# A hybrid decoder layer on eight cores: the first steps of stage2 are moved into the stage3 before it

## The chip, the cores and the metric

The kernel runs on all eight cores of one Trainium2 chip. Each core takes one prompt sequence (2048 tokens, width 1024) and 16 of the 128 sample tokens; the cores exchange nothing. The metric is the device time of the slowest core in microseconds (us).

## What is computed

The layer normalises x (RMS), projects it with w_in, runs a gated linear attention (GLA) branch and a Mamba-2 (SSD) branch over the sequence, merges them with sigmoid gates, applies w_out, adds x and normalises again. Cut to what matters here:

```
hn = rmsnorm(x, norm_g); q,k,v,g,a_lr,z,xbc,dt_raw,gate_a,gate_b = split(hn @ w_in)
log_a = log_sigmoid(a_lr @ w_a2 + b_a2) / 16        # per key channel
o, S = gla_recurrence(q/8, k, v, log_a, S0)         # S_t = diag(a_t) S_{t-1} + k_t^T v_t, o_t = q_t S_t
o = rmsnorm(o) * silu(g)
x_s, B, C = silu(causal_conv(xbc, width 4)); dt = softplus(dt_raw + dt_bias)
y, h = ssd_recurrence(x_s, dt, -exp(a_log), B, C, h0)   # h_t = exp(dt_t A) h_{t-1} + dt_t x_t B_t^T
y = rmsnorm((y + d_skip * x_s) * silu(z))
merged = sigmoid(gate_a) * (o @ w_br_gla) + sigmoid(gate_b) * (y @ w_br_ssd)
out = rmsnorm(x + merged @ w_out)
```

## The kernel before, in words

The 2048 tokens of a core are eight super-chunks (s = 0 to 7) of SC = 256 tokens, each of two chunks (ci = 0, 1) of 128. All of a super-chunk's work lies in generators that record instructions; a `yield` ends a step. The recorded order is the order of each engine's queue (PE, ACT, DVE, POOL, SP), and a wait is added where a named tile was last written or read on another engine. Readers of one PSUM bank (`pb0` to `pb6`) wait for each other too. Nothing is reordered later.

- `stage1a(s)` (L488), 23 steps: for both 128-token tiles the Square of x (ACT), the rstd and xn (POOL), the transposes (PE), xnT (DVE); then the `alr` projection, `wa2`, Exp and Ln to `eb`, the dt projection with its Exp and Ln, `latok` and four scans to `bpos` (DVE, L546), two Exps to `eb` and `enb`, then the k and q projections, each with a product on DVE.
- `stage1b(s)` (L566), 40 steps: six times projection, copy to `xbc_raw` (ACT), convolution in the single buffer `cacc` (four DVE instructions), Silu (ACT): 24 steps; then g and z, four projections with a Silu each: 16 steps.
- `stage2(s)` (L605): `chunk_gen(0)`, then `chunk_gen(1)`, of 8 steps each. Step 1: the V projection, `vtok`, `ktok`, `ccol`. Step 2: cumulative sums over `tri_f` on PE, the differences to `tmp4` and `tg` (eight DVE instructions), Exp to `decay` and `rs`. Step 3: `xdt`, `Btok`, `scm`. Step 4: the two masked products `ATm` (a half of `scrB`). Step 5: the GLA output (`scrB` x `vtok` and `qtT` x `S_bf`, called bo), `sq`, `t1`, the state `S_f`, `S_bf`, and Ln and Exp of the norm in place in a bank (bsg). Step 6: `CsT`, the two `Mg`, `xw`, `ogT`. Step 7: the SSD output (by), y to `tg`, the state `hT_f`. Step 8: the product with z, the norm, `ygT`.
- `stage3_m(s)` (L753), 8 steps (m = 0 to 7): 16 gate and 8 branch matmuls, Tanh to `tg` (ACT), the product (DVE), the sum to `mrgT` (POOL). `tg` is a single buffer.
- `stage3_tail(s)` (L776), 6 steps: two with 16 `wout` matmuls each and the residual on `xr`; then for both tiles the Square and rstd, and the final product with the store of `yp`.

`interleave(gp, gf, rp, rf)` takes rp steps of the first and rf steps of the second in turn. Stage2(s) is woven with tail(s-1) and stage1a(s+1), 1 to 2; stage3(s) with stage1b(s+1), 1 to 5. Ahead of s=0, `late_weights` queues eight weight transfers on POOL, of which each waits for the sixth before it. All matmuls are recorded at L220, transposes at L228, ACT at L234, DVE at L239, L248 and L253, copies at L260, transfers at L272. In the text V is the V projection of chunk 0, and a name with an apostrophe (V', bo', CsT') is the same thing in chunk 1.

Of the kernel before, what the change touches and what calls it, by code (L numbers as in the profile page):

```python
# [9 lines left out]
AF = mybir.ActivationFunctionType  # L10
# [269 lines left out]
def build_program(with_sample=True, stop=None):  # L280
# [18 lines left out]
    with ExitStack() as st:  # L299
# [305 lines left out]
        def stage2(s):  # L605
# [13 lines left out]
            def chunk_gen(ci):  # L619
                sl = slice(ci * 128, (ci + 1) * 128)  # L620
                vn = "vtok%d" % ci
                b, bn = bank(pool=POOL_B)
                k.mmg([(b[:, :], xs_[:, kc, sl], w_in_bf[:, kc, C_V:C_V + 512], kc == 0, kc == 7) for kc in range(8)],
                      wres(C_V, C_V + 512) + [xsn], [bn])
                k.cp("act", vtok[:, ci, :], b[:, :], [bn], [vn])
                ptk = pt[:, 0:256]
                k.trg([(ptk[:, cc * 128:(cc + 1) * 128], k_[:, cc, sl], ident_bf[:]) for cc in range(2)], [kn, "ident_bf"], ["pt"])
                k.cp("act", ktok[:, :], ptk, ["pt"], ["ktok"])
                bc_, bcn = bank(pool=POOL_B)
                k.mmg([(bc_[:, 0:8], tri_f[:, :], la_[:, ci, :], True, True)], ["tri_f", lan], [bcn])  # L630
                k.ts("dve", ccol[:, :], bc_[:, 0:8], -1.0, None, ALU.mult, None, [bcn], ["ccol"])
                yield
                for g in range(2):
                    pr = slice(64 * g, 64 * g + 64)
                    bcu, bcun = bank(pool=POOL_B)
                    bcuv = v4(bcu[:, :], 4)
                    k.mmg([(bcuv[:, hh, :], la_[:, ci, 4 * g + hh:4 * g + hh + 1].broadcast_to([128, 128]), tri_f[:, :], True, True)
                           for hh in range(4)], [lan, "tri_f"], [bcun])
                    for hh in range(4):
                        k.ts("dve", diffs[g][:, hh, :], bcuv[:, hh, :], ccol[:, 4 * g + hh:4 * g + hh + 1], 0.0, ALU.add, ALU.min,  # L640
                             [bcun, "ccol"], [diffn[g]])
                    k.act(decay[:, 4 * g:4 * g + 4, :], diffs[g], AF.Exp, [diffn[g]], ["decay%d" % g])
                    k.act(expcum[pr, :, :], bcuv[pr, :, :], AF.Exp, [bcun], ["rs%d" % g])
                yield
                bx, bxn = bank(pool=POOL_B)
                k.trg([(bx[:, cc * 128:(cc + 1) * 128], x_[:, cc, sl], ident_f[:]) for cc in range(4)], [xsn_, "ident_f"], [bxn])
                k.tt("dve", xdt[:, :, :], bx[:, :].rearrange("p (h q) -> p h q", h=8),
                     dt_[:, ci, :].unsqueeze(2).broadcast_to([128, 8, 64]), ALU.mult, [bxn, dtn], ["xdt"])
                ptb = pt[:, 256:384]
                k.trg([(ptb, B_[:, sl], ident_bf[:])], [Bn, "ident_bf"], ["pt"])  # L650
                k.cp("act", Btok[:, :], ptb, ["pt"], ["Btok"])
                for g in range(2):
                    pr = slice(64 * g, 64 * g + 64)
                    bsc, bscn = bank(pool=POOL_B)
# [37 lines left out]
                k.cp("act", S_bf[:, :, :], S_f[:, :, :], ["S_f"], ["S_bf"])
                bsg, bsgn = bank(hold=True, pool=POOL_B)
                k.mmg([(bsg[:, :], ones_bf[:, :], sq[:, :, :].rearrange("p h i -> p (h i)"), True, True)], ["ones_bf", "sq"], [bsgn])
                k.act(bsg[:, :], bsg[:, :], AF.Ln, [bsgn], [bsgn], scale=1.0 / 128, bias=EPS)
                k.act(bsg[:, :], bsg[:, :], AF.Exp, [bsgn], [bsgn], scale=-0.5)
                yield
                k.tt("dve", CsT[:, :, :], expcum[:, :, :], C_[:, sl].unsqueeze(1).broadcast_to([128, 4, 128]), ALU.mult,
                     ["rs0", "rs1", Cn], ["CsT"])
                for g in range(2):  # L700
                    k.tt("dve", Mgs[g], decay[:, 4 * g:4 * g + 4, :], scm[:, g, :].unsqueeze(1).broadcast_to([128, 4, 128]), ALU.mult,
                         ["decay%d" % g, "scm%d" % g], [Mgn[g]])
                k.tt("dve", xw[:, :, :], xdt[:, :, :], decay[:, :, 127:128].broadcast_to([128, 8, 64]), ALU.mult,
                     ["xdt", "decay0", "decay1"], ["xw"])
                k.tt("dve", ogT[:, :, sl].rearrange("p (cc hh) i -> p hh cc i", hh=2),
                     t1[:, :, :].rearrange("p (hh cc) i -> p hh cc i", hh=2),
                     v4(bsg[:, :], 4).rearrange("p (hh cc) i -> p hh cc i", hh=2), ALU.mult, ["tmp4", bsgn], ["ogT"])
                release(bsgn)
                yield
                bh, bhn = bank(hold=True, pool=POOL_B)  # L710
                bhv = bh[:, 0:256].rearrange("p (h q) -> p h q", h=4)
                for g in range(2):
                    pr = slice(64 * g, 64 * g + 64)
                    by, byn = bank(pool=POOL_B)
                    byv = by[:, 0:256].rearrange("p (c i) -> p c i", c=2)
                    mms = []
                    for hh in range(4):
                        h = 4 * g + hh
                        po = byv[64 * (h % 2):64 * (h % 2) + 64, hh // 2, :]
                        mms.append((po, xdt[:, h, :], Mgs[g][:, hh, :], True, False))  # L720
                        mms.append((po, hT_bf[pr, hh, :], CsT[pr, hh, :], False, True))
# [28 lines left out]
            for ci in range(2):  # L750
                yield from chunk_gen(ci)
# [479 lines left out]
```

How the kernel before makes its waits and increments, by code:

```python
        def replay(ename, eng):  # L155
            mysem = sems[ename]
            for o in ops[ename]:
                for (k, v) in o.waits:
                    eng.wait_ge(sems[k], v)
                if o.dma_key is not None:
                    instrs = o.fn(eng)
                    assert len(instrs) == o.dma_n, (len(instrs), o.dma_n)
                    for ins in instrs:
                        ins.then_inc(sems[o.dma_key], 16)
                elif o.fn is None:
                    eng.nop().then_inc(mysem, 1)
                else:
                    ins = o.fn(eng)
                    ins.then_inc(mysem, 1)
```

## Time and profile before

| | |
|---|---|
| median of 3 runs | 1128.01 us (1125.84 to 1129.49) |
| the profiled execution | 1125.68 us |
| its slowest core (5), span | 1124.1 us; cores 1114.6 to 1124.1 |
| granted PE clock, mean | 0.747 of full |
| busy: PE, PE weight load | 691.3 us (61%), 470.8 us (42%) |
| busy: DVE, ACT, POOL | 497.9 (44%), 312.4 (28%), 153.1 (14%) |
| chain that ended last | PE 39%, DVE 26%, issue 14%, ACT 10%, DMA 5%, POOL 4% |

In time the eight super-chunks fill about 60 to 950 us of the span, the sample batch the rest. The profile in 40 slices (28.1 us each) shows the pattern that repeats:

```profile
PE   0645788468846884688468846884788468140025
DVE  1424552555255525552555255535552442124762
PEclk9965699569956995699569956995699569565557
```

### The profile page before, as it was taken

The page shows a single profiled execution, that of the slowest core. Times are in us where ns is not written, and L with a number is a line of the kernel's source. Part 1 is how long each engine was busy: PE and PEld are TensorE (multiplying, and loading weights), DVE is VectorE, ACT ScalarE, POOL GpSimd, SP SyncE. Part 2 cuts the span into 40 slices and gives each one's busy share as a digit, 9 for nine tenths or more (in the row PEclk, how much of TensorE's full clock was granted, in tenths as well). Part 3 has the DMA queues.
Part 4 walks back from the last instruction along what each step waited for, and adds up shares of the span by engine and source line. Part 5 has one row for each costly group of instructions (what it writes and reads, how often), then busy time and mean ns, then how long its engine had stood idle before and what let it go on. Part 6 is the DMA issues. An engine that isn't in the chain of part 4 may idle for free.

```text
span 1124.1 us, 14666 instructions; the slowest of 8 cores (1114.6 to 1124.1 us)
## 1 busy us (share of the span) xinstructions
PE 691.3 (61%) x4703; PEld 470.8 (42%) x4703; DVE 497.9 (44%) x1029; ACT 312.4 (28%) x662; POOL 153.1 (14%) x232
## 2 busy tenths in 40 slices
PE   0645788468846884688468846884788468140025
PEld 0432476247624752475247624752475245020001
DVE  1424552555255525552555255535552442124762
ACT  1232232332233223322332233323332332020001
POOL 4021210201020102010201020102010002102221
PEclk9965699569956995699569956995699569565557
DMA  9989400300030003000300030002000200401420
GB/s 141 161 102 199 75 2 1 113 1 1 1 112 1 1 1 113 1 1 1 113 0 1 2 112 1 1 1 75 1 1 1 75 6 1 119 18 31 133 75 3
DMA packets 29612, 50.54 MB, mean 45 GB/s; under 512 B 7098, under 2 KB 18973, under 8 KB 29536
## 3 DMA queue, kind: packets, MB, share of 16 engines
q0 software_dynamic: 17968, 22.60, 11.6%
q1 hardware_dynamic: 10160, 22.80, 6.5%
q10 hardware_dynamic: 1408, 4.20, 1.3%
q8 instruction: 39, 0.64, 0.2%
q14 instruction: 37, 0.30, 0.1%
HBM read 50.60 MB, written 13.30 MB: 57 GB/s over the span
## 4 chain that ended last, share of the span: by engine, by line
PE 39%; DVE 26%; issue 14%; ACT 10%; DMA 5%; POOL 4%; DVEq 1%; SPq 1%; ACTq 0%; POOLq 0%
PE pb L220 38%; DVE cacc L253 7%; DMA w_in_bf<-w_in 3%; ACT tg L234 2%; DVE xnT L239 2%; DVE cacc L248 2%; DVE tmp L248 2%; DVE tg L253 1%; ACT sq L234 1%; DVE scrB L239 1%; PE pt L228 1%; POOL sm L239 1%; DVE xr L239 1%; DVEq L159 1%; ACT L234 1%
## 5 line engine op out<-in xcount | busy, mean ns | idle before, releaser
L220 PE MATMUL pb<-xnT,w_in_bf 128*128 128x256 bf16 (+1 forms) x2240 | 316.2, 304 | 50.3 <-ACT gs L234 23.8
L220 PEld LDWEIGHTS pb<-xnT,w_in_bf 128*128 128x128 bf16 (+1 forms) x2240 | 237.6, 108 | 111.1 <-issue 62.3
L253 DVE SCALAR_TENSOR_TENSOR tg<-tg,pb 128x512 f32<-128x512 f32 (+1 forms) x66 | 45.3, 687 | 153.6 <-ACT tg L234 83.3
L239 POOL TENSOR_TENSOR mrgT<-tg 128x256 bf16<-128x256 f32 x64 | 46.8, 732 | 398.0 <-DVE tg L253 393.9
L253 DVE SCALAR_TENSOR_TENSOR cacc<-xbc_raw,prm,cacc 128x256 f32<-128x256 f32 x144 | 77.6, 539 | 15.6 <-DVE cacc L253 0.5
L220 PE MATMUL pb<-scrB,vtok 128*128 128x128 bf16 x64 | 18.0, 281 | 74.1 <-DVE scrB L239 74.1
L234 ACT ACTIVATE tg<-pb 128x512 f32<-128x512 f32 (+1 forms) x68 | 40.1, 590 | 71.5 <-PE pb L220 57.0
L228 PE MATMUL pt<-ident_bf,xn 128*128 128x128 bf16 (+1 forms) x144 | 17.3, 294 | 67.7 <-POOL xn L245 63.0
L220 PE MATMUL pb<-wout,mrgT 128*128 128x512 bf16 x256 | 56.5, 379 | 2.2 <-POOL mrgT L239 2.2
L234 ACT ACT_TABLE_LOAD x20 | 25.7, 1283 | 112.7 <-DVE tmp L248 64.7
L220 PE MATMUL pb<-sq,ones_bf 128*128 128x128 bf16 (+1 forms) x80 | 18.7, 357 | 59.7 <-ACT sq L234 59.7
L220 PE MATMUL pb<-scrB,xdt 128*64 128x128 bf16 x128 | 36.4, 284 | 20.7 <-DVE scrB L239 20.7
L220 PE MATMUL pb<-w_in_bf,xnT 128*128 128x8 bf16 (+1 forms) x256 | 47.4, 331 | 0.0
L228 PEld LDWEIGHTS pt<-ident_bf,xn 128*128 128x128 bf16 (+1 forms) x144 | 13.7, 136 | 71.8 <-issue 71.3
L220 PEld LDWEIGHTS pb<-scrB,vtok 128*128 128x128 bf16 x64 | 6.7, 105 | 84.0 <-issue 78.5
L253 DVE SCALAR_TENSOR_TENSOR xr<-xr,sm,fng_rep 128x1024 f32<-128x1024 f32 x16 | 20.6, 1284 | 44.6 <-POOL sm L239 44.6
L253 DVE SCALAR_TENSOR_TENSOR xr<-pb,xr 128x512 f32<-128x512 f32 x32 | 22.1, 692 | 40.0 <-PE pb L220 40.0
L220 PE MATMUL pb<-ogT,wbrg 128*128 128x256 bf16 x256 | 39.1, 276 | 0.0
L220 PE MATMUL pb<-ygT,wbrs 128*128 128x256 bf16 x256 | 38.9, 275 | 0.0
L234 ACT ACTIVATE xsT<-cacc 128x256 f32<-128x256 f32 x32 | 13.3, 416 | 90.1 <-DVE cacc L253 90.1
L220 PEld LDWEIGHTS pb<-wout,mrgT 128*128 128x128 bf16 x256 | 25.0, 100 | 30.8 <-issue 2.4
L220 PE MATMUL pb<-CsT,hT_bf 64*64 64x128 bf16 x128 | 36.5, 285 | 0.0
(201 smaller groups left out, 1064.4 us busy)
## 6 DMA issues: line engine op xcount, KB each, us to landing
xt<-xp SPq DMA_DIRECT2D x16, 512.0 KB, 4.5
xr<-xp SPq DMA_DIRECT2D x16, 512.0 KB, 4.6
yp<-xr POOLq DMA_DIRECT2D x16, 512.0 KB, 3.1
w_in_bf<-w_in POOLq DMA_DIRECT2D x7, 1024.0 KB, 33.3
wout<-w_out POOLq DMA_DIRECT2D x2, 1024.0 KB, 45.7
w_in_bf<-w_in POOLq DMA_DIRECT2D x2, 768.0 KB, 26.3
w_in_bf<-w_in POOLq DMA_DIRECT2D x2, 512.0 KB, 15.1
wbrg<-w_br_gla POOLq DMA_DIRECT2D x1, 1024.0 KB, 43.8
```

The costliest lines, as they stand in the source:

```text
L159: eng.wait_ge(sems[k], v)
L220: ins = e.matmul(o, lhsT=l, rhs=r, start=s0, stop=s1)
L228: ins = e.transpose(o, i, idn)
L234: return e.activation(out=out, in_=in_, func=func, **kw)
L239: return e.tensor_tensor(out=out, in0=in0, in1=in1, op=op)
L248: return e.tensor_scalar(out=out, in0=in0, scalar1=s1, scalar2=s2, op0=op0, op1=op1)
L253: return e.scalar_tensor_tensor(out=out, in0=in0, scalar=scalar, in1=in1, op0=op0, op1=op1)
```

## The change

`chunk_gen` takes a `part`. "pre" is steps 1, 2 and 4, "post" is the others (3, 5, 6, 7, 8), "all" is all eight as before. `stage2(s, pre_only=True)` records the pre part of chunk 0; `stage2(s)` records its post part and the whole of chunk 1. In "pre" the second group of differences goes to `bpos` instead of `tg`, which stage3 uses. For s=0 the pre part stands by itself after stage1b(0), ahead of `late_weights`. For the others it is chained behind stage1b(s+1) in the weave with stage3(s), whose ratio goes from 1:5 to 1:6. The rest of the diff is indentation.

```
-        def stage2(s):
+        def stage2(s, pre_only=False):
...
-            def chunk_gen(ci):
+            def chunk_gen(ci, part="all"):
...
+                PRE = (1, 2, 4)
+                dfs = [diffs[0], bpos[:, :, :].rearrange("p a (b c) -> p (a b) c", c=128)] if part != "all" else diffs
+                dfn = [diffn[0], "bpos"] if part != "all" else diffn
+                if part == "all" or (part == "pre") == (1 in PRE):
...
+                if part == "all" or (part == "pre") == (2 in PRE):
...
+                            k.ts("dve", dfs[g][:, hh, :], bcuv[:, hh, :], ccol[:, 4 * g + hh:4 * g + hh + 1], 0.0, ALU.add, ALU.min,
+                                 [bcun, "ccol"], [dfn[g]])
+                        k.act(decay[:, 4 * g:4 * g + 4, :], dfs[g], AF.Exp, [dfn[g]], ["decay%d" % g])
...
-            for ci in range(2):
-                yield from chunk_gen(ci)
+            if pre_only:
+                yield from chunk_gen(0, "pre")
+            else:
+                yield from chunk_gen(0, "post")
+                yield from chunk_gen(1, "all")
...
             interleave(g1a, stage1b(0), 2, 1)
+            run(stage2(0, pre_only=True))
             late_weights()
...
-                    interleave(stage3_m(s), stage1b(s + 1) if nxt else iter(()), 1, 5)
+                    interleave(stage3_m(s), chain(stage1b(s + 1), stage2(s + 1, pre_only=True)) if nxt else iter(()), 1, 6)
```

## Rows read from the trace of the kernel before

**Rows 1.** Stretches of one super-chunk: length, busy us of each engine, PE clock, DMA.

```profile
407.59:431.47 23.88, 12.18 (x73) 6.91 (x71) 9.98 (x20) 8.37 (x15) 2.58 (x7) 0.82 0.06 23
431.47:449.91 18.44, 11.97 (x61) 6.35 (x62) 10.15 (x21) 5.46 (x12) 3.98 (x7) 0.50 0.40 143
449.91:469.45 19.54, 14.33 (x92) 8.76 (x92) 9.18 (x28) 7.45 (x17) 0.19 (x1) 0.67 0.00 1
469.45:481.36 11.91, 8.50 (x50) 5.51 (x48) 6.66 (x16) 3.11 (x7) 0.00 (x0) 0.65 0.00 1
481.36:520.10 38.74, 33.62 (x291) 28.81 (x289) 17.67 (x32) 12.12 (x28) 5.91 (x9) 0.96 0.00 1
```

**Rows 2.** Timeline of PE: start, length (us), instruction, [idle before, releaser].

```profile
407.59 1.89 PE L220 MATMUL pb<-w_in_bf,xnT 128*128 128x512 bf16 x8
...
409.62 7.07 PE L220 MATMUL pb<-wout,mrgT 128*128 128x512 bf16 x32
416.53 1.95 PE L220 MATMUL pb<-tri_f,latok 128*128 128x128 f32 x16
...
431.47 0.27 PE L220 MATMUL pb<-scrB,vtok 128*128 128x128 bf16 x1 [7.92 <-DVE scrB L239]
```

**Rows 3.** Timeline of DVE: final product 0, a product of ATm, CsT.

```profile
425.44 1.28 DVE L253 SCALAR_TENSOR_TENSOR xr<-xr,sm,fng_rep 128x1024 f32<-128x1024 f32 x1 [4.38 <-POOL sm L239]
...
430.38 0.95 DVE L239 TENSOR_TENSOR scrB<-pb,mask_bf 128x256 bf16<-128x256 f32 x2
...
436.64 0.68 DVE L239 TENSOR_TENSOR CsT<-rs,CT 128x512 bf16<-128x512 f32 x1
```

**Rows 4.** Timeline of ACT, and last the xn of POOL.

```profile
419.50 1.28 ACT L234 ACT_TABLE_LOAD   x1 [9.05 <-DVE tmp L248]
420.79 0.63 ACT L234 ACTIVATE decay<-tmp 128x512 bf16<-128x512 f32 x1
...
423.06 1.06 ACT L234 ACTIVATE mrgT<-xr 128x1024 bf16<-128x1024 f32 x1
...
435.94 1.25 ACT L234 ACTIVATE pb<-pb 128x512 f32<-128x512 f32 x2
437.11 1.05 ACT L234 ACTIVATE xn<-xt 128x1024 bf16<-128x1024 f32 x1
...
439.52 1.12 POOL L245 TENSOR_SCALAR xn<-xt,sm 128x1024 bf16<-128x1024 f32 x1 [0.18 <-POOL sm L239]
```

**Rows 5.** Stretches of 4 us in stage3 of s=3, columns as in rows 1.

```profile
392.00:396.00 4.00, 0.79 (x8) 0.48 (x6) 2.19 (x4) 1.56 (x4) 0.78 (x2) 0.97 0.00 0
396.00:400.00 4.00, 4.00 (x24) 2.98 (x23) 0.25 (x1) 0.38 (x1) 0.72 (x1) 0.60 0.01 2
```

**Rows 6.** Timeline of DVE: the first instruction of three convolutions.

```profile
496.64 0.41 DVE L248 TENSOR_SCALAR cacc<-xbc_raw,prm 128x256 f32<-128x256 f32 x1 [1.01 <-ACT xbc_raw L234]
...
499.83 0.67 DVE L248 TENSOR_SCALAR cacc<-xbc_raw,prm 128x256 f32<-128x256 f32 x1 [0.41 <-ACT xbc_raw L234]
...
504.05 0.41 DVE L248 TENSOR_SCALAR cacc<-xbc_raw,prm 128x256 f32<-128x256 f32 x1
```

**Rows 7.** Timelines: scans in chunk 1, table load, tanh and sum of m=0.

```profile
461.01 2.00 DVE L546 TENSOR_TENSOR_SCAN bpos<-ones_f,eb 128x128 f32<-128x128 f32 x4
...
481.66 1.28 ACT L234 ACT_TABLE_LOAD   x1 [2.34 <-PE pb L220]
482.95 0.60 ACT L234 ACTIVATE tg<-pb 128x512 f32<-128x512 f32 x1
...
484.57 0.76 POOL L239 TENSOR_TENSOR mrgT<-tg 128x256 bf16<-128x256 f32 x1 [20.52 <-DVE tg L253]
```

**Rows 8.** Timelines of s=0: transposes of xn, xnT, V' and CsT'.

```profile
85.59 1.01 PE L228 MATMUL pt<-ident_bf,xn 128*128 128x128 bf16 x8 [13.28 <-POOL xn L245]
...
86.71 1.23 DVE L239 TENSOR_TENSOR xnT<-pt,prm 128x1024 bf16<-128x1024 bf16 x1 [11.75 <-PE pt L228]
...
113.70 2.96 PE L220 MATMUL pb<-w_in_bf,xnT 128*128 128x512 bf16 x8
...
128.83 0.69 DVE L239 TENSOR_TENSOR CsT<-rs,CT 128x512 bf16<-128x512 f32 x1
```

More of the change, by code:

```diff
@@ new lines, in chunk_gen @@
+                if part == "all" or (part == "pre") == (3 in PRE):
+                    bx, bxn = bank(pool=POOL_B)
+                    k.trg([(bx[:, cc * 128:(cc + 1) * 128], x_[:, cc, sl], ident_f[:]) for cc in range(4)], [xsn_, "ident_f"], [bxn])
+                    k.tt("dve", xdt[:, :, :], bx[:, :].rearrange("p (h q) -> p h q", h=8),
+                         dt_[:, ci, :].unsqueeze(2).broadcast_to([128, 8, 64]), ALU.mult, [bxn, dtn], ["xdt"])
+                    ptb = pt[:, 256:384]
+                    k.trg([(ptb, B_[:, sl], ident_bf[:])], [Bn, "ident_bf"], ["pt"])
+                    k.cp("act", Btok[:, :], ptb, ["pt"], ["Btok"])
+                    for g in range(2):
+                        pr = slice(64 * g, 64 * g + 64)
+                        bsc, bscn = bank(pool=POOL_B)
+                        k.mmg([(bsc[:, 0:128], B_[pr, sl], C_[pr, sl], True, True)], [Bn, Cn], [bscn])
+                        k.tt("dve", scm[:, g, :], bsc[:, 0:128], mask_bf[:, :], ALU.mult, [bscn, "mask_bf"], ["scm%d" % g])
+                    yield
@@ new lines, in chunk_gen @@
+                if part == "all" or (part == "pre") == (4 in PRE):
+                    ATv = ATm.rearrange("p (cc hh) i -> p hh cc i", hh=2)
+                    for hh in range(2):
+                        pr = slice(64 * hh, 64 * hh + 64)
+                        ba, ban = bank(pool=POOL_B)
+                        bav = ba[:, 0:256].rearrange("p (c i) -> p c i", c=2)
+                        k.mmg([(bav[:, cc, :], k_[pr, cc, sl], q_[pr, cc, sl], True, True) for cc in range(2)], [kn, qn], [ban])
+                        k.tt("dve", ATv[:, hh, :, :], bav, mask_bf[:, :].unsqueeze(1).broadcast_to([128, 2, 128]), ALU.mult,
+                             [ban, "mask_bf"], ["ATm"])
+                    yield
@@ new lines, in chunk_gen @@
+                if part == "all" or (part == "pre") == (5 in PRE):
+                    for hh in range(2):
+                        pr = slice(64 * hh, 64 * hh + 64)
+                        bo, bon = bank(pool=POOL_B)
+                        bov = bo[:, 0:256].rearrange("p (c i) -> p c i", c=2)
+                        mms = []
+                        for cc in range(2):
+                            h = 2 * cc + hh
+                            mms.append((bov[:, cc, :], vtok[:, ci, h * 128:(h + 1) * 128], ATm[:, h, :], True, False))
+                            mms.append((bov[:, cc, :], S_bf[pr, cc, :], q_[pr, cc, sl], False, True))
+                        k.mmg(mms, [vn, "ATm", "S_bf", qn], [bon])
+                        k.act(sq[:, 2 * hh:2 * hh + 2, :], bov, AF.Square, [bon], ["sq"])
+                        for cc in range(2):
+                            k.tt("dve", t1[:, 2 * hh + cc, :], g_[:, 2 * cc + hh, sl], bov[:, cc, :], ALU.mult, [bon, gn], ["tmp4"])
+                    bk, bkn = bank(pool=POOL_B)
+                    bkv = bk[:, 0:256].rearrange("p (c e) -> p c e", c=2)
+                    mms = []
+                    for hh in range(2):
+                        for cc in range(2):
+                            h = 2 * cc + hh
+                            mms.append((bkv[64 * hh:64 * hh + 64, cc, :], ktok[:, cc * 128 + hh * 64:cc * 128 + hh * 64 + 64],
+                                        vtok[:, ci, h * 128:(h + 1) * 128], True, True))
+                    k.mmg(mms, ["ktok", vn], [bkn])
+                    k.tt("dve", S_f[:, :, :], S_f[:, :, :], bkv, ALU.add, ["S_f", bkn], ["S_f"])
+                    k.tt("dve", S_f[:, :, :], S_f[:, :, :], ebl[pb][:, :, ci:ci + 1].broadcast_to([128, 2, 128]), ALU.mult,
+                         ["S_f", "ebl" + sfx], ["S_f"])
+                    k.cp("act", S_bf[:, :, :], S_f[:, :, :], ["S_f"], ["S_bf"])
+                    bsg, bsgn = bank(hold=True, pool=POOL_B)
+                    k.mmg([(bsg[:, :], ones_bf[:, :], sq[:, :, :].rearrange("p h i -> p (h i)"), True, True)], ["ones_bf", "sq"], [bsgn])
+                    k.act(bsg[:, :], bsg[:, :], AF.Ln, [bsgn], [bsgn], scale=1.0 / 128, bias=EPS)
+                    k.act(bsg[:, :], bsg[:, :], AF.Exp, [bsgn], [bsgn], scale=-0.5)
+                    yield
@@ new lines, in chunk_gen @@
+                if part == "all" or (part == "pre") == (6 in PRE):
+                    k.tt("dve", CsT[:, :, :], expcum[:, :, :], C_[:, sl].unsqueeze(1).broadcast_to([128, 4, 128]), ALU.mult,
+                         ["rs0", "rs1", Cn], ["CsT"])
+                    for g in range(2):
+                        k.tt("dve", Mgs[g], decay[:, 4 * g:4 * g + 4, :], scm[:, g, :].unsqueeze(1).broadcast_to([128, 4, 128]), ALU.mult,
+                             ["decay%d" % g, "scm%d" % g], [Mgn[g]])
+                    k.tt("dve", xw[:, :, :], xdt[:, :, :], decay[:, :, 127:128].broadcast_to([128, 8, 64]), ALU.mult,
+                         ["xdt", "decay0", "decay1"], ["xw"])
+                    k.tt("dve", ogT[:, :, sl].rearrange("p (cc hh) i -> p hh cc i", hh=2),
+                         t1[:, :, :].rearrange("p (hh cc) i -> p hh cc i", hh=2),
+                         v4(bsg[:, :], 4).rearrange("p (hh cc) i -> p hh cc i", hh=2), ALU.mult, ["tmp4", bsgn], ["ogT"])
+                    release(bsgn)
+                    yield
@@ new lines, in chunk_gen @@
+                if part == "all" or (part == "pre") == (8 in PRE):
+                    k.tt("dve", y1_, y1_, z_[:, :, sl], ALU.mult, ["tg", zn], ["tg"])
+                    k.act(sq[:, :, :], y1_, AF.Square, ["tg"], ["sq"])
+                    bs, bsn = bank(hold=True, pool=POOL_B)
+                    bsv = bs[:, 0:256].rearrange("p (g i) -> p g i", g=2)
+                    mms = []
+                    for g in range(2):
+                        mms.append((bsv[:, g, :], ones_bf[:, :], sq[:, 2 * g, :], True, False))
+                        mms.append((bsv[:, g, :], ones_bf[:, :], sq[:, 2 * g + 1, :], False, True))
+                    k.mmg(mms, ["ones_bf", "sq"], [bsn])
+                    k.act(bsv, bsv, AF.Ln, [bsn], [bsn], scale=1.0 / 256, bias=EPS)
+                    k.act(bsv, bsv, AF.Exp, [bsn], [bsn], scale=-0.5)
+                    k.tt("dve", ygT[:, :, sl].rearrange("p (g t) i -> p g t i", g=2), y1_.rearrange("p (g t) i -> p g t i", g=2),
+                         bsv.unsqueeze(2).broadcast_to([128, 2, 2, 128]), ALU.mult, ["tg", bsn], ["ygT"])
+                    release(bsn)
+                    yield
```

170 lines of the change are left out of this document (45 added, 125 removed).

## The prediction, written before the changed kernel was run

> **What bounds the kernel now.** I read the chain of waits first: no engine is full, PE is busy 61% and DVE 44% of the span, and the chain runs through PE 39%, DVE 26%, "issue" 14% and ACT 10%. So the time is set by hand-overs, in the order in which each engine's instructions were written out. The stretch view then says where. Five stretches of one super-chunk (s=4's stage2 and stage3) run from one V projection to the next [rows 1]: A, from V to the first `scrB x vtok` matmul (bo), 23.88; B, bo to the V projection of chunk 1 (V'), 18.44; C, V' to CsT of chunk 1 (CsT'), 19.54; D, CsT' to the first `ogT x wbrg` matmul of stage3, 11.91; E, the rest of stage3, 38.74. Together 112.5 us, and the other super-chunks repeat it. In E PE is busy 33.6 of 38.7 us at a clock of 0.96. In A to D it is busy half to three quarters of the time at 0.50 to 0.82: latency chains. Last I read the timelines of A on PE, DVE, ACT and POOL for who waits for whom [rows 2 to 4].
>
> **The change, part by part.** Nothing is removed from the work. Steps 1, 2 and 4 of chunk 0 (V, ktok, ccol; decay; ATm) go behind m=6 and m=7 of the stage3 before. stage3 now takes 6 filler steps an m instead of 5, so stage1b's 40 steps end inside m=6, and m=7's 24 projection matmuls come after V. stage2 has 13 own steps instead of 16 against the same 29 filler steps (6 of the tail, 23 of stage1a). I walk the same five stretches, time 0 at the start of V.
>
> A. V, ktok and bc as now; the cumulative matmuls (bcu), now queued behind the 32 wout matmuls, start at 2.03, where wout starts now [rows 2]. From bcu to the table load before Exp is 2.97 (416.53 to 419.50), load and four Exps hold ACT 3.56 (419.50 to 423.06) [rows 2, 4]: ACT is free at 8.56. m=7's tanh is queued behind them; tanh, DVE's product and POOL's sum take 2.38 (482.95 to 485.33) [rows 7], so mrgT is whole at 10.9 and wout can start at about 11.0. Now it starts at 2.03 and never waits. It takes 6.9 at full clock [rows 2] and ends at 17.9. PE has little to do from 6.5 on, which costs clock: after a window with 0.79 us of work PE was granted 0.60 on average, so about 3.2 us of 4 at the half level, although it was dense again [rows 5]. A like dip under wout costs 1.9: bo at 19.8. The ends: 17.9 (no dip) and 24.5 (all of wout at half clock). Today's tail of the chain (final product 0, the wait for it 4.38, final product 1, ATm) [rows 3] no longer stands ahead of bo. A: 23.9 to 19.8, a gain of 4.1, with m=7 inside it.
>
> B. From bo to the end of bsg's Exp is 5.7 now (431.47 to 437.19) [rows 2, 4]. Ahead of its Ln stands a table load that is new, 1.28 [rows 4], because tanh ran since the Exps: 6.9, or 6.6 with bo's matmuls at full clock. Only then comes the Square of the final norm, moved from A; Square to final product 0 is 2.38 (423.06 to 425.44), the product 1.2 more [rows 3, 4]. CsT stands behind it on DVE: at 10.1 instead of 5.2 (431.47 to 436.64). Final product 1 goes in ahead of the y products (1.2), hT and the product with z end at about 17.5. stage1a's Square of x stands before sq on ACT; from that Square (16.9 or so) to xn is 3.5 (437.11 to 440.64) [rows 4], V' is behind the transposes of xn, 1.0 more: 22.0. Against it, the alr projection and the second transposes, which are ahead of V' today, move to C. Ends 20.7 (load hidden) and 23.3. B: 18.4 to 22.0.
>
> C. The second xn, its transposes and DVE's 1.2 us copy, the alr projection and wa2 now stand between V' and ATm', each short, the waits alr to wa2 to ATm' on PE among them: but diffs' end is about as late as now, and bo' comes at 13.4 instead of 15.2. Then stage1a's dt Exp and Ln and the 2.0 us of scans [rows 7], which ran ahead of xdt' in time that ends at bo', stand between S_f and CsT': CsT' 8.4 after bo' rather than 4.3. Ends 19.5 and 23. C: 19.5 to 21.8.
>
> D. k1, q0 and q1 are left when step 8 is done; q0 and q1 (8 matmuls each, 0.9 at full and 1.8 at half clock) stand alone ahead of stage3's m=0, q1 waiting for k1's product on DVE. That is 2.5, and by' at half clock 1.0. Ends 13.5 and 17. D: 11.9 to 15.4.
>
> E. Six convolutions share one buffer cacc. Between two of them is 3.2 us without a tanh (496.64 to 499.83) and 4.2 with one (499.83 to 504.05) [rows 6]. After: 3 gaps with and 2 without, plus one more copy in the first, 19.9; now 19.7 from the first to the last. So four m's lie under the convolutions where five did, PE only idles more, and the m=7 that left E for A is given back. E: 38.7 to 38.9; ends 37.7 and 41.
>
> Sum of a period: 19.8 + 22.0 + 21.8 + 15.4 + 38.9 = 117.9, against 112.5: **+5.4**. Six whole periods (s=1 to 6): +32.4.
>
> s=0: V does not wait for stage3, and late_weights holds POOL's queue, so PE stood 13.28 us for xn [rows 8]. Steps 3 and 5 now run ahead of that stand. DVE goes from xnT (87.9 [rows 8]) to CsT, y, xnT, the product with z by 97.2; the ones, alr and wa2 matmuls follow, V' at 101.5 instead of 113.70: -12.2. But V' to CsT' was 15.1 there (113.70 to 128.83) because scan and dt were already done; it becomes the 19.5 of C today. s=0: -7.8, with E's +0.2: -7.6. Ends -11 and -3. s=7 has no stage1a: A -4.1, CsT 4.9 later, final product 1 inside: +1.7.
>
> Total: 32.4 - 7.6 + 1.7 = +26.5 on the profiled execution's 1125.7: 1152.2. The median of the three runs is 2.3 above that execution, so **1154.5**. No DMA is added; the xt and xr loads and the yp stores land in about 5 us in the bands where they are issued and nothing waits for them.
>
> **Table loads.** Two loads a super-chunk today, before decay's Exp and before stage3's tanh [rows 4, 7]. I add one. Whether m=7's tanh, right after the Exps, needs another no row shows: 0 or 1.28. I take 0, since the loads of this kernel each serve a mixed run (Exp with Ln, tanh with Silu), and keep 1.28 as a rival. The Trainium skill (ScalarE: Activation LUTs, section Table sets: the hidden batching unit) puts exp and tanh in one set and exp and ln in another; by that, it is three loads a super-chunk, as summed. The same section has a rule against this change: batch calls by set, not by function. The section What ACT_TABLE_LOAD costs gives about 2.66 us a switch, load and drain together. The trace shows 1.28 and the Exp directly behind it (419.50 to 420.79) [rows 4]; by the page's price the added switch would cost 1.4 us a period more.
>
> **The rivals.** (1) Faster: the moved work falls into idle time. DVE is busy 10.15 of 18.44 us in B and 9.18 of 19.54 in C [rows 1]; if final norm, xn, alr and scans fit there without holding CsT, only A's -4.1, the new load's 1.3 and E's 0.2 remain, -2.6 a period: 6 x -2.6 - 7.6 - 2.8 = -26, 1102. Against it: engines take their queue in order, and B, C and D gain instructions ahead of the ones on the chain. It decides where B, C and D together grow by less than about 5 us instead of 9.3. (2) Slower than forecast: the tanh of m=7 takes a load too, and wout runs wholly at half clock: 1.3 and 4.9 a period, seven times: 1198; the load alone 1163. (3) No change: the pre-work moves only past m=7, one m of eight, and what it saves in A comes back in B to D one for one: 1128.
>
> **How the numbers follow.** Forecast 0.58, a load more (with or without the clock) 0.12, the faster rival 0.21, no change 0.09. The ends of a period are about -3 and +16 if all fall one way; that they do is unlikely, and -2 to +9 gives -18 to +54 in all. Range 1110 to 1182, which leaves the faster rival's core outside. A measurement of this kernel can tell about 0.3% from no change: faster 0.23, same 0.08, slower 0.69.
>
> **What would show it.** wout waiting for POOL's mrgT and starting some 11 us after V; three table loads a period, the new one before bsg's Ln; final product 0 right ahead of CsT with an idle wait for POOL's sm; scans between S_f and CsT' in chunk 1; q0 and q1 alone before stage3; the convolution stretch as long as now; in s=0 V' some 12 us earlier. It is wrong if CsT comes under 8 us after bo, if the period is 112 or less, or if the convolutions shorten with the denser fill.

## The result, and the profile after

The changed kernel takes **1172.5 us** (median of 10 runs), the kernel before 1126.7 in the same comparison: a ratio of **1.041** (95% interval 1.039 to 1.042), slower by 46 us. 1154.5 was forecast, with a range of 1110 to 1182: the side held and so did most of the mechanism, but the rise was 1.7 times the forecast one. In a few executions one die showed a lower clock and took longer: they are left out of every ratio, they hardly move the medians (the move with placed fillers at 1:5 is 1093.3 without its one), and the experiment with two of them in four (the filler pair behind step 6) is told by the other two.

From the page of the changed kernel: its span, the chain of waits by engine, wout's row (56.5 us before, with 2.2 of waiting), and the table loads (20 before).

```profile
span 1171.0 us, 14690 instructions; the slowest of 8 cores (1160.5 to 1171.0 us)
...
PE 38%; DVE 24%; issue 13%; ACT 12%; POOL 5%; DMA 5%; DVEq 1%; SPq 1%; ACTq 0%; POOLq 0%
...
L220 PE MATMUL pb<-wout,mrgT 128*128 128x512 bf16 x256 | 70.2, 443 | 8.0 <-POOL mrgT L239 8.0
L234 ACT ACT_TABLE_LOAD x27 | 34.6, 1283 | 90.6 <-PE pb L220 37.4
```

The same matmuls are there (4703), seven table loads more, one for each of s=1 to 7; ACT's share in the chain is 12% instead of 10%, POOL's 5% instead of 4%. The five stretches of the super-chunk that answers to [rows 1], with columns as there. (By the count of V projections it is s=3, before as after; the prediction called it s=4, and [rows 5], which name s=3, lie in stage3 of s=2. No number hangs on it.)

```profile
420.52:440.47 19.95, 16.82 (x98) 9.68 (x95) 7.40 (x18) 5.64 (x10) 0.86 (x2) 0.91 0.00 0
440.47:462.76 22.29, 7.84 (x45) 4.28 (x44) 10.98 (x22) 8.54 (x16) 4.92 (x9) 0.62 0.12 48
462.76:486.52 23.76, 15.01 (x96) 8.27 (x94) 10.96 (x29) 9.10 (x20) 1.86 (x3) 0.64 0.27 90
486.52:501.89 15.37, 12.27 (x63) 7.55 (x64) 7.39 (x18) 2.93 (x6) 0.45 (x1) 0.55 0.00 0
501.89:540.22 38.33, 31.72 (x267) 26.33 (x264) 16.82 (x31) 11.74 (x27) 5.09 (x8) 0.91 0.00 1
```

A is shorter than its 23.88; B, C and D are longer than 18.44, 19.54 and 11.91; E is about the same. PE's clock in E fell from 0.96 to 0.91. Over s=1 to 6, from the start times of the same instructions in the timelines (us, means of six):

| | A | B | C | D | E | period |
|---|---|---|---|---|---|---|
| before | 23.9 | 18.4 | 19.7 | 12.0 | 38.8 | 112.7 |
| forecast | 19.8 | 22.0 | 21.8 | 15.4 | 38.9 | 117.9 |
| after | 20.4 | 22.3 | 23.6 | 15.5 | 39.0 | 120.8 |

The table is of the slowest core of each execution; the period of every other core is within 0.2 us of it. Six such periods make +48.4, s=0 gives -6.5, s=7 +2.5, the time up to the first V +2.2, the end +0.3: together the 46.9 by which the spans differ.

The rows that decide, PE first (V, wout, bo, V', the second transposes, the alr projection, wa2, bo'), then DVE (final product 0, CsT, and in chunk 1 the last differences, scans and CsT'), then ACT:

```profile
420.52 1.89 PE L220 MATMUL pb<-w_in_bf,xnT 128*128 128x512 bf16 x8
...
431.88 8.75 PE L220 MATMUL pb<-wout,mrgT 128*128 128x512 bf16 x32 [0.82 <-POOL mrgT L239]
440.47 0.22 PE L220 MATMUL pb<-scrB,vtok 128*128 128x128 bf16 x1
...
462.76 3.62 PE L220 MATMUL pb<-w_in_bf,xnT 128*128 128x512 bf16 x8
...
471.12 0.61 PE L228 MATMUL pt<-ident_bf,xn 128*128 128x128 bf16 x8 [2.57 <-POOL xn L245]
...
473.21 0.27 PE L228 MATMUL pt<-ident_bf,BT 128*128 128x128 bf16 x1 [1.04 <-DVE xnT L239]
...
473.62 1.87 PE L220 MATMUL pb<-xnT,w_in_bf 128*16 128x256 bf16 x8
476.11 0.58 PE L220 MATMUL pb<-alr,wa 16*128 16x256 bf16 x2 [0.61 <-ACT alr L234]
...
478.22 0.26 PE L220 MATMUL pb<-scrB,vtok 128*128 128x128 bf16 x1 [0.68 <-DVE dtt L239]
```

```profile
449.50 1.28 DVE L253 SCALAR_TENSOR_TENSOR xr<-xr,sm,fng_rep 128x1024 f32<-128x1024 f32 x1 [5.36 <-POOL sm L239]
450.70 0.69 DVE L239 TENSOR_TENSOR CsT<-rs,CT 128x512 bf16<-128x512 f32 x1
...
469.48 1.72 DVE L248 TENSOR_SCALAR tg<-pb,ccol 128x128 f32<-128x128 f32 x4
...
484.60 2.00 DVE L546 TENSOR_TENSOR_SCAN bpos<-ones_f,eb 128x128 f32<-128x128 f32 x4
486.52 0.67 DVE L239 TENSOR_TENSOR CsT<-rs,CT 128x512 bf16<-128x512 f32 x1
```

```profile
425.68 1.28 ACT L234 ACT_TABLE_LOAD   x1 [2.30 <-DVE tmp L248]
...
428.62 0.59 ACT L234 ACTIVATE rs<-pb 64x512 f32<-64x512 f32 x1
429.24 0.60 ACT L234 ACTIVATE tg<-pb 128x512 f32<-128x512 f32 x1
...
444.67 1.28 ACT L234 ACT_TABLE_LOAD   x1
```

wout, which started 2.03 after V [rows 2], starts 11.36 after it, waits for the last mrgT, and takes 8.6 instead of 6.9. m=7's tanh (start 429.24) stands behind the four Exps with no load between. CsT stands behind final product 0, which waited 5.36 for POOL; in [rows 3] the wait for POOL (4.38) lay in A. The scans stand right ahead of CsT'.

### The profile page after: what moved, and what is told of

It reads as the page before. It is cut to its first block, busy times and chain, and to the rows that moved or that the text cites. A ratio compares the mean times of both kernels' runs of the same rounds, so it can differ in the third digit from the quotient of the medians.

```text
span 1171.0 us, 14690 instructions; the slowest of 8 cores (1160.5 to 1171.0 us)
## 1 busy us (share of the span) xinstructions
PE 721.0 (62%) x4703; PEld 473.4 (40%) x4703; DVE 500.0 (43%) x1029; ACT 322.5 (28%) x669; POOL 159.0 (14%) x232
## 4 chain that ended last, share of the span: by engine, by line
PE 38%; DVE 24%; issue 13%; ACT 12%; POOL 5%; DMA 5%; DVEq 1%; SPq 1%; ACTq 0%; POOLq 0%
PE pb L220 37%; DVE cacc L253 6%; DMA w_in_bf<-w_in 3%; ACT tg L234 2%; DVE tg L253 2%; ACT L234 2%; DVE cacc L248 2%; PE pt L228 2%; DVE xnT L239 1%; ACT pb L234 1%; POOL xn L245 1%; POOL sm L239 1%; DVE xr L239 1%; DVE bpos L546 1%; DVE S_f L239 1%
## 5 line engine op out<-in xcount | busy, mean ns | idle before, releaser
L220 PE MATMUL pb<-xnT,w_in_bf 128*128 128x256 bf16 (+1 forms) x2240 | 325.3, 309 | 63.3 <-ACT xbc_raw L234 39.3
L220 PE MATMUL pb<-scrB,xdt 128*64 128x128 bf16 x128 | 39.2, 306 | 95.0 <-DVE scrB L239 94.9
L220 PE MATMUL pb<-wout,mrgT 128*128 128x512 bf16 x256 | 70.2, 443 | 8.0 <-POOL mrgT L239 8.0
L228 PE MATMUL pt<-ident_bf,xn 128*128 128x128 bf16 (+1 forms) x144 | 14.5, 262 | 78.3 <-POOL xn L245 69.3
L220 PEld LDWEIGHTS pb<-scrB,xdt 128*64 128x64 bf16 x128 | 16.5, 129 | 111.6 <-issue 100.6
L234 ACT ACT_TABLE_LOAD x27 | 34.6, 1283 | 90.6 <-PE pb L220 37.4
L234 ACT ACTIVATE tg<-pb 128x512 f32<-128x512 f32 (+1 forms) x68 | 40.2, 591 | 63.1 <-PE pb L220 48.4
L220 PEld LDWEIGHTS pb<-wout,mrgT 128*128 128x128 bf16 x256 | 28.0, 111 | 47.7 <-issue 27.2
L228 PEld LDWEIGHTS pt<-ident_bf,xn 128*128 128x128 bf16 (+1 forms) x144 | 11.1, 120 | 82.6 <-issue 82.6
L248 POOL TENSOR_SCALAR sm<-ss 128x1 f32<-128x1 f32 (+2 forms) x36 | 10.0, 278 | 249.3 <-ACT mrgT L234 128.4
L220 PE MATMUL pb<-CsT,hT_bf 64*64 64x128 bf16 x128 | 39.5, 309 | 0.0
L234 ACT ACTIVATE xsT<-cacc 128x256 f32<-128x256 f32 x32 | 13.3, 416 | 93.8 <-DVE cacc L253 93.7
L220 PE MATMUL pb<-ygT,wbrs 128*128 128x256 bf16 x256 | 38.9, 275 | 0.0
## 6 DMA issues: line engine op xcount, KB each, us to landing
w_in_bf<-w_in POOLq DMA_DIRECT2D x2, 512.0 KB, 16.9
```

The lines of the kernel that those rows point to most:

```text
L220: ins = e.matmul(o, lhsT=l, rhs=r, start=s0, stop=s1)
L228: ins = e.transpose(o, i, idn)
L234: return e.activation(out=out, in_=in_, func=func, **kw)
L248: return e.tensor_scalar(out=out, in0=in0, scalar1=s1, scalar2=s2, op0=op0, op1=op1)
```

## The experiments

All times are medians; stretches are means over s=1 to 6 as in the table above, and the kernel before took 1125 to 1126 us in each comparison.

**The stage3 ratio in the changed kernel.**

```
-  interleave(stage3_m(s), chain(stage1b(s + 1), stage2(s + 1, pre_only=True)) if nxt else iter(()), 1, 6)
+  interleave(stage3_m(s), chain(stage1b(s + 1), stage2(s + 1, pre_only=True)) if nxt else iter(()), 1, 5)
```

> The changed kernel with the stage3 weave back at 1:5, so that the pre part follows m=7 instead of lying around it. My theory: wout (now 11.4 us after V) waits for m=7's tanh, which stands behind the four Exps, and the new table load before bsg's Ln is there only because of that tanh. With m=7 ahead of V both go: two loads a super-chunk, wout some 8 us after V, bound by the bank that the second Exp to rs frees, so A about 17 us instead of 20.4; B 1.3 shorter (21.0); E, from stage3's first branch matmul to V, stays at about 39, since it is then one m longer but five m's lie under the convolutions again. Period about 116, total about 1172.5 - 7 x 4.5 = 1141. Rival (the pre part gains because m=7 is inside it): E grows by the 2.6 us of m=7, and the total stays within 5 us of the changed kernel.

Measured 1143.7, a ratio of 1.017 (1.015 to 1.019). A 18.2, B 20.9, C 23.1, D 15.4, E 39.5. wout starts 9.2 after V, the loads are two again. Expected and measured agree within 3 us, though A was to be 17. So 29 of the 46 us go with the ratio. Of the 3.7 us of a period, A gives 2.2 and B 1.4, the two places where m=7's tanh made itself felt. ACT after V in this kernel: the Exps are followed by Btok, and no load stands between S_bf and bsg's Ln (from the start of S_bf to that of Ln is 0.32 us; in the changed kernel it is 1.73, and that is the 1.4 us of B).

```profile
417.46 0.59 ACT L234 ACTIVATE rs<-pb 64x512 f32<-64x512 f32 x1
418.07 0.28 ACT L234 ACTIVATE Btok<-pt 128x128 bf16<-128x128 bf16 x1
...
430.90 0.42 ACT L234 ACTIVATE S_bf<-S_f 128x256 bf16<-128x256 f32 x1 [1.89 <-DVE S_f L239]
431.22 1.25 ACT L234 ACTIVATE pb<-pb 128x512 f32<-128x512 f32 x2
```

**The ratio alone, in the kernel before.** `..., 1, 5)` becomes `..., 1, 6)`.

> The kernel before with the stage3 weave at 1:6 and nothing else. My theory: the six convolutions take the same 20 us whatever lies beside them, so with 6 fillers an m only four m's lie under them; m=7's 2.6 us of matmuls then come alone at the end, E grows from 38.8 to about 41.3, total +2.5 x 7 = +17, 1144. Rival (denser filling shortens the convolution part or fills idle PE time): E the same or shorter, total 1127 or less.

Measured 1149.7, ratio 1.022 (1.021 to 1.024): slower by 25 where 17 was expected, A to D within 0.4 of the kernel before, E 38.8 to 41.7. The convolutions on DVE (first instruction of each of the six, s=3) took 20.0 from the first to the last start, as [rows 6] let expect (19.7 from 484.33 to 504.05 before):

```profile
494.73 0.41 DVE L248 TENSOR_SCALAR cacc<-xbc_raw,prm 128x256 f32<-128x256 f32 x1
...
499.25 0.41 DVE L248 TENSOR_SCALAR cacc<-xbc_raw,prm 128x256 f32<-128x256 f32 x1
...
502.74 0.41 DVE L248 TENSOR_SCALAR cacc<-xbc_raw,prm 128x256 f32<-128x256 f32 x1 [1.01 <-ACT xbc_raw L234]
...
506.75 0.41 DVE L248 TENSOR_SCALAR cacc<-xbc_raw,prm 128x256 f32<-128x256 f32 x1
...
511.34 0.41 DVE L248 TENSOR_SCALAR cacc<-xbc_raw,prm 128x256 f32<-128x256 f32 x1
...
514.76 0.41 DVE L248 TENSOR_SCALAR cacc<-xbc_raw,prm 128x256 f32<-128x256 f32 x1 [0.96 <-ACT xbc_raw L234]
```

So denser filling does not shorten them, and E grew by about the 2.6 us of one m's matmuls. (Here the ratio costs E; in the changed kernel it cost A and B. The two prices are near each other, but they are not the same one.)

**The new table load alone, in the kernel before.**

```
+                if ci == 0:
+                    k.act(dumt[:, :], ccol[:, :], AF.Tanh, ["ccol"], ["dumt"])
```

> The kernel before with one more ScalarE instruction: a tanh of 128x8 values of ccol into an unused tile, after the ATm step of chunk 0. It forces the table load before bsg's Ln that the change brought, at the same place, and nothing else. My theory: the load is on the chain (Ln, Exp, Square, ...), three loads a super-chunk; but here CsT does not wait for bsg on DVE, only ogT, the fourth of DVE's next products does, and the Square of x: so 1.3 us at most, about 1.0 us a period, total +8, 1135. If the load is hidden: within 2 us of before. If a switch costs 2.66 us as the Trainium skill says (ScalarE: Activation LUTs, What ACT_TABLE_LOAD costs): +19.

Measured 1127.5, ratio 1.001 (0.998 to 1.003). The loads are there, 28 instead of 20, right ahead of Ln (ACT, s=3), and B is 18.4 as before: hidden. My 8 us were wrong.

```profile
438.30 0.42 ACT L234 ACTIVATE S_bf<-S_f 128x256 bf16<-128x256 f32 x1 [1.80 <-DVE S_f L239]
438.73 1.28 ACT L234 ACT_TABLE_LOAD   x1
440.02 1.26 ACT L234 ACTIVATE pb<-pb 128x512 f32<-128x512 f32 x2
```

The load costs what hangs behind it. Here that is ogT and the Square of x, which have slack: every wait of PE in B is as long as before. In the changed kernel it is the Square of the final norm and so CsT, and there B is 22.3 with the load and 20.9 without (the run at 1:5). Ln starts directly behind the load. A switch of 2.66 us, as the Trainium skill has it (ScalarE: Activation LUTs, What ACT_TABLE_LOAD costs), is not seen. The sets of the Trainium skill (the same page, Table sets: the hidden batching unit), exp with tanh in one and exp with ln in another, do agree with the trace of the changed kernel, where tanh follows Exp with no load (429.24) and Ln takes one (444.67).

**Fillers dealt so that chunk 1 meets the same ones as before.**

```
+  weave(stage2(s), chain(tail_prev, stage1a(s + 1) if nxt else iter(())), [2, 4, 4, 4] + [2] * 9 if s else [2] * 13)
```

(`weave` takes one step of stage2, then as many fillers as the list says.)

> The changed kernel with the fillers of stage2 for s>0 dealt out 2, 4, 4, 4, 2 over the five own steps left of chunk 0 and 2 after each step of chunk 1, so that chunk 1 meets the same fillers as in the kernel before (scans ahead of bo', q and k products under step 8). My theory: C falls from 23.6 to 19.7 and D from 15.5 to 12.1, and B grows by the second transposes, the alr projection and the wa2 step, about 4 to 5 us, to 27; per period -3, total about 1172.5 - 6 x 3 = 1154. Rival (fillers cost the same wherever they stand): within 5 us of the changed kernel. Rival (chunk 0's longer filler blocks stand in front of the chain): B over 31 and slower than 1172.

Measured 1208.3, ratio 1.077 (1.072 to 1.082). C 19.0 and D 11.6, as expected; B 36.6, where 27 was expected: the rival with the long blocks held. PE, s=3, from chunk 0's norm on, the two rows with the long waits:

```profile
467.25 1.01 PE L228 MATMUL pt<-ident_bf,xn 128*128 128x128 bf16 x8 [15.64 <-POOL xn L245]
...
478.46 1.01 PE L228 MATMUL pt<-ident_bf,xn 128*128 128x128 bf16 x8 [5.74 <-POOL xn L245]
```

Two blocks of four held Square, xn, transposes and xnT in a row. The first transposes are queued on PE ahead of step 7's matmuls and wait there for ACT and POOL, and stage2 with them. The block before, with both final products, also stands ahead of CsT, which comes 13.9 after bo instead of 10.2. What a filler costs is not its count but what it waits for while own steps are queued behind it.

**One filler pair moved behind step 6, in the changed kernel.** The list is `[2, 0, 4] + [2] * 10`.

> The changed kernel with one filler pair of stage2 moved for s>0: fillers dealt 2, 0, 4, 2, 2, ..., so that final product 0 and its Square come after step 6 of chunk 0 instead of ahead of it. My theory: what holds CsT at 10.23 us after bo is final product 0 ahead of it on DVE (Ln's table load, Ln, Exp, Square, rstd, product in a row). CsT then comes at about 5 us, but both final products and their rstd waits now stand in one block ahead of the y products, so V' gains only part: B 22.3 to 19 or 20; C, D, E as they are; total about 1172.5 - 6 x 2.5 = 1157. Rival (CsT is held by S_f and PE's clock, not by the product): CsT over 9 and the total unchanged. Rival from the run with blocks of four fillers: the block costs more than it frees, B over 23.

Measured 1162.3 and 1164.0. CsT comes 3.6 after bo instead of 10.2, which shows what held it; B falls only from 22.3 to 21.5, since the products then stand ahead of the y products. I had expected 1157 and a third to a half of the freed 6.6 us to reach V'; an eighth did. More of the 9 us came from C, 22.4 instead of 23.6, which I had not expected; why is not shown.

**The final norm split, in the kernel before.** Squares and rstds in their own columns after steps 2 and 3, the products after steps 5 and 6; stage1a's fillers as before.

```
+  weave(stage2(s), tail_prev, stage1a(s + 1) if nxt else iter(()), ["tt", "t", "t", "aa", "taa", "taa"] + ["aa"] * 10)
```

(t is a step of the tail, a one of stage1a; s=0 keeps its 1:2.)

> The kernel before with only the tail's last four fillers changed: both Squares and rstds stand after steps 2 and 3 of chunk 0, on a column of their own each, and the two final products with their stores after steps 5 and 6; stage1a's fillers stand where they do in the kernel before. My theory: in A, DVE's xdt, scm and ATm wait behind final products for POOL's rstd (4.38 and 1.46 us idle, 2.6 us busy). With them away ATm ends some 6 to 7 us sooner, A 23.9 to 17.5; B gets the two products (2.5) and the Squares' effect on sq, 18.4 to 21.5; C, D, E as before; per period -3 to -4, total 1127 - 7 x 3.5 = 1102. Rival (A is bound by the Exps and the banks they free on PE, not by DVE): A over 21, and the total slower than before because B has grown.

Measured **1098.8**, ratio 0.976 (0.975 to 0.978). A 16.5, B 21.9, C 19.7, D 12.1, E 38.9. Against [rows 3] DVE goes from the differences through xdt and scm to ATm with no wait for POOL (s=3):

```profile
411.33 1.72 DVE L248 TENSOR_SCALAR tg<-pb,ccol 128x128 f32<-128x128 f32 x4
412.96 0.68 DVE L239 TENSOR_TENSOR xdt<-pb,dtt 128x512 bf16<-128x512 f32 x1
413.56 0.48 DVE L239 TENSOR_TENSOR scm<-pb,mask_bf 128x128 bf16<-128x128 f32 x2
414.41 0.42 DVE L239 TENSOR_TENSOR scrB<-pb,mask_bf 128x256 bf16<-128x256 f32 x1 [0.38 <-PE pb L220]
415.64 0.42 DVE L239 TENSOR_TENSOR scrB<-pb,mask_bf 128x256 bf16<-128x256 f32 x1 [0.80 <-PE pb L220]
...
421.20 1.28 DVE L253 SCALAR_TENSOR_TENSOR xr<-xr,sm,fng_rep 128x1024 f32<-128x1024 f32 x1
```

A falls by 7.3, more than the move of three steps brought (3.5), and B pays 3.5 of it. The total came 3 us below the 1102 expected.

**Stage3 at 1:4, on the split final norm.**

> The kernel with the split final norm (1098.8 us, period 109.2) with the stage3 weave at 1:4 instead of 1:5. My theory of E: the six convolutions take about 20 us whatever lies beside them, so more m's under them shortens the rest. At 1:6 four m's lay there and E grew by 2.9 in the kernel before; at 1:4 six lie there, E 38.9 to 36.5 to 37.5 (the extra m's product lengthens the convolutions by up to 1), total 1098.8 - 7 x 1.9 = 1085. Rival (1:5 is the balance point: beyond it the convolutions become the longer side because each m puts a tanh and a product in their chain): E 39 or more, total 1098 or slower.

Measured **1071.4**, ratio 0.952 (0.947 to 0.956). E falls from 38.9 to 34.6, twice what I had expected. All five gaps between convolutions now hold a tanh (first and last start, s=3, 21.4 apart), yet six m's lie under them. The window is E of s=4.

```profile
460.71 0.41 DVE L248 TENSOR_SCALAR cacc<-xbc_raw,prm 128x256 f32<-128x256 f32 x1
...
482.10 0.41 DVE L248 TENSOR_SCALAR cacc<-xbc_raw,prm 128x256 f32<-128x256 f32 x1
...
563.33:597.90 34.57, 32.32 (x289) 27.99 (x289) 17.92 (x32) 12.04 (x28) 5.97 (x9) 1.00 0.00 1
```

Against E in [rows 1], PE's idle time falls from 5.1 to 2.3 us and its busy time from 33.6 to 32.3, for the same matmuls: that is the whole gain. The granted clock is 1.00 (2.4 GHz) against 0.96. The longest wait behind the last convolution shows both; first the kernel before, then this one:

```profile
507.93 4.45 PE L220 MATMUL pb<-xnT,w_in_bf 128*128 128x256 bf16 x24 [3.21 <-ACT gs L234]
...
485.98 1.91 PE L220 MATMUL pb<-xnT,w_in_bf 128*128 128x256 bf16 x16 [0.59 <-ACT gs L234]
```

After the 3.21 us, 24 matmuls take 4.45 us (PE was granted 0.57 of full over 508 to 512 us); elsewhere in E 24 of them take 2.78. At 1:4 no wait of PE in E is longer than 1.2 us. What sets E changes with it. The chain of waits within E of s=3, by line, before and at 1:4:

```profile
by line: PE pb L220 32.1%; DVE cacc L253 26.1%; issue 15.8%; ACT tg L234 7.4%; DVE cacc L248 7.2%; ACT L234 3.3%; ACT xbc_raw L234 2.9%; DVEq L159 1.7%; DVE tg L253 1.3%; ACTq L159 1.1%; ACT gs L234 0.7%; ACT xsT L234 0.4%; ACT BT L234 0.1%
...
by line: PE pb L220 82.6%; DVE cacc L253 5.2%; issue 4.5%; ACT tg L234 3.4%; ACT gs L234 1.9%; DVE cacc L248 1.2%; DVE tg L253 0.4%; DVEq L159 0.4%; ACTq L159 0.3%; ACT CT L234 0.1%
```

Before, the convolutions hold a third of the chain; at 1:4 the matmuls hold four fifths, so most of what this ratio can give is taken. A ratio of 1:3 was not tried.

**The move with placed fillers, stage3 at 1:5.** The changed kernel with the split norm and the plan

```
+  ["ttaa", "ttaaaa", "taa", "taa", "aa"] + ["aa"] * 8
```

> The changed kernel with stage3 at 1:5 (as in the run at 1143.65) and the fillers of stage2 placed by what they wait for: Square and xn of x under wout, both Squares of the final norm and both transposes spread, the final products after steps 6 and 7, the alr, wa2, eb and dt steps ahead of V', two a step in chunk 1. My theory: the move itself costs nothing; it lost because 13 own steps cover fewer fillers in the 1:2 weave. Then A 17.8, B 22.5, C 19.5 and D 12.2 as before the change, E 39.3: period 111, total about 1143.65 - 6 x 5.5 = 1110, faster than the kernel before by 1.4%, but slower than the split final norm without the move (1098.8), whose A is 16.4. Rival (the move loses because wout now starts 9 us after V and the Exps hold ACT, whatever the fillers do): total 1130 or more.

Measured **1094.4**, ratio 0.971 (0.967 to 0.976), 16 us below what I had expected, and 49 us less than the changed kernel at the same ratio, by the places of the fillers and the split alone. A 17.9, B 23.0, C 17.6, D 12.4, E 38.7. C is shorter than in any kernel without the move, and here the eb and dt projection steps, too, are recorded ahead of V'; bo' comes 13.3 after it instead of 15.3. The rival is out, and a kernel with the move can be faster than the kernel before. That the move itself costs nothing is not shown: the split alone, without the move, is as fast (the two intervals overlap), A is 1.4 longer here than there, and the same placing of stage1a's fillers without the move was not tried.

**The same at 1:4, and the changed kernel at 1:4.**

> The kernel with the move, stage3 at 1:5 and placed fillers (1094.4 us) with stage3 at 1:4. If E's gain (38.9 to 34.6 in the kernel without the move) is the convolutions' own and independent of what follows stage3: E 34.6, A, B, C, D as at 1:5 (17.7, 23.0, 17.6, 12.4), period 105.4, total 1094.4 - 7 x 4.3 = 1064, 5.5% faster than before and about equal to the one without the move (1071.4). Rival (the last fillers and the pre part pile up behind m=7, so A grows): total 1075 or more.

Measured **1068.4**, ratio 0.950 (0.948 to 0.952), the lowest time of all: A 18.2, B 23.1, C 17.3, D 12.4, E 35.3 (34.4 to 35.0 but for one super-chunk at 38.5, in which PE was busy throughout and was granted 0.80). That is 4 us more than expected, and 3 less than without the move (1071.4), where the intervals of the two ratios overlap.

> The changed kernel with the stage3 weave at 1:4 and nothing else: third point of the series 1:6 (1172.5), 1:5 (1143.65). Theory: a period's E goes from 39.3 to 34.8, A, B, C, D stay as at 1:5 (18.1, 20.9, 23.1, 15.4), total 1143.65 - 7 x 4.4 = 1113: the ratio then accounts for more of the changed kernel's loss than the move. Rival (E's gain comes only where A to D are short): 1130 or more.

Measured 1109.5, ratio 0.987 (0.985 to 0.989), E 34.5. The changed kernel with one number altered is 1.3% faster than the kernel before, which stands at 1:5; at 1:4 that one is the faster, as the next run shows.

**The kernel before at 1:4**, the last cell:

> The kernel before with the stage3 weave at 1:4 and nothing else, the last cell of a table of three ratios with and without the move: before 1149.7 at 1:6, 1125 at 1:5; with the move 1172.5, 1143.7, 1109.5. Theory: ratio and move add up. E 38.8 to 34.6, A, B, C, D as before, total 1125 - 7 x 4.2 = 1096, and the move costs 14 at 1:4 where it costs 19 at 1:5 and 23 at 1:6. Rival (the move is worth something once the ratio is right): this kernel at 1109 or more.

Measured 1099.4, ratio 0.977 (0.976 to 0.979), E 34.4. The rival is out, the move still costs, but ratio and move do not simply add up: I had expected it to cost 14 here, and it costs 10. The table (us; the last column holds the split norm in both kernels, and placed fillers of stage1a only with the move):

| stage3 ratio | without the move | with it, fillers 1:2 | the move | split norm: with the move, without |
|---|---|---|---|---|
| 1:6 | 1149.7 | 1172.5 | +22.8 | |
| 1:5 | 1125.3 | 1143.7 | +18.4 | 1094.4 with, 1098.8 without |
| 1:4 | 1099.4 | 1109.5 | +10.1 | 1068.4 with, 1071.4 without |

From 1125.3 to 1172.5, the ratio gives +24.4 and the move with its 1:2 fillers +22.8 if the ratio is changed first; with the move first they give +28.8 and +18.4.

## Why the prediction was right, and where it was short

- **A** (19.8, measured 20.4): wout was to start 11.0 after V and started 11.4; bo's time hangs on it. The loss of clock was there: PE was granted 0.80 under wout, which took 8.6, so 1.7 more than at full clock. I had put 1.9 for it, but the 3.2 us at the half level that I read from [rows 5] cost only 1.6. In s=1, 2 and 6 A was 0.8 to 1.0 longer than in the others.
- **B** (22.0, measured 22.3): the order Ln's load, Ln, Exp, Square, rstd, product, CsT held row by row; CsT was 10.2 after bo where 10.1 was forecast. That the load has a price only there is shown by the two runs on it. That V' fits so well is in part luck: the steps named from the Square of x on (16.9, 3.5, 1.0) add up to 21.4 and not to 22.0, and that Square came at 17.8.
- **C** (21.8, measured 23.6) is the term that was mis-sized, by 1.8 a period and 11 us in all. The step that failed is "bo' comes at 13.4 instead of 15.2": it came at 15.2, as before. The forecast took away the 2.0 us of scans, which had stood ahead of xdt' and bo', and gave no price to what came in their place, though it lists it all. The end of the differences was about as late as before (8.4 after V', 9.0 before), as forecast; from there to bo' 7.0 us passed, where the forecast left about 4.4. In them the transposes of B, which share the tile `pt` with those of xn, wait for the xnT copy (1.04), the alr projection behind them takes 1.87 at a granted clock of 0.50 (as it did before, but then ahead of V'), and wa2 waits for alr's copy (0.61), all ahead of the matmuls of ATm'. The second half of C, 8.3 from bo' to CsT' with the scans in it, held (8.4).
- **D** (15.4, measured 15.5) and **E** (38.9, measured 39.0) held. In the kernel before E is 41.7 at 1:6, 38.8 at 1:5 and 34.4 at 1:4. At 1:6 and 1:5 the convolutions and the number of m's under them account for it, as I had it; at 1:4 PE's own work does. I had set the ratio's cost in E against the m=7 that left it, which was right for E, but I never asked what the ratio costs in all: the runs put about half of the whole loss to it.
- **s=0** -6.5 (-7.6), **s=7** +2.5 (+1.7, of which the two terms with a number, -4.1 and +4.9, give only 0.8). The first V came 2.2 later, in a stretch in which the two kernels do the same; within one execution the cores already differ there by 4 us before (64.9 to 69.0) and 5 after (64.9 to 70.4), and the two profiles are of different cores (5 and 3).
- **The range.** Its upper end, +54, leaves out the -5.9 of s=0 and s=7 that its lower end holds; with them it is 1176, and the measured time still lies inside.
- **The rivals.** The rival with one load more is out: there is none before m=7's tanh, so three loads a super-chunk. "Faster, because the moved work falls into idle time" failed as the change stood. With placed fillers its condition was met, B, C and D together grew by 3 instead of 11 over before, and the kernel was faster than before; the limit of 5 us that I had worked out fits both. But that kernel also has the split norm, which alone gives as much. The third rival, that what A saves comes back one for one, fell short: A's gain of 3.5 was lost to B alone, and C and D came on top.

What stays open: of the 49 us between the two kernels with the move at 1:5, how much the split norm gives and how much the placing of stage1a's steps. They were not tried apart. Nor was that placing tried without the move, so whether the move is worth anything by itself is open too.

## What to carry to other kernels

When steps are moved out of one weave into another, count what is left on both sides: fillers per own step, and what each filler waits for while own steps are queued behind it. Put an instruction that waits for a far engine (a rstd, a normalised tile) one to three own steps behind the one that starts it, and not as its neighbour. And read the ratio of a weave as the place of a chain (here six convolutions through one buffer) in the other work: putting more of that work beside the chain shortens the stage until the other engine is full, here at 1:4. When a change alters such a ratio on the way, try the ratio alone: here that one number made about half of the result.

## What the runs showed of the hardware that I had not expected

- A table load of 1.28 us right ahead of an Ln cost nothing measurable in one order of work (ratio 1.001, 0.998 to 1.003) and 1.4 us a period in another, by what was queued behind it on ACT.
- E's gain at 1:4 was 4.3 us, more than the 2.6 of one m's matmuls: PE's granted clock over the stretch went from 0.96 (0.91 in the changed kernel) to 1.00. In the kernel before, the 3.21 us wait of PE was followed by 24 matmuls in 4.45 us instead of 2.78, although PE was dense again; two waits of 0.6 us in its place cost no clock.
